# Sparse attention on one core: index keys, head weights and keys as one 328-column product with the tokens stationary

## What is computed

```python
proj = x @ w_in                                   # x: 256 x 1024, w_in: 1024 x 2120
q, k, v, iq, ik, iw = split(proj)                 # 1024, 256, 256, 512, 64, 8 columns
q, k, iq, ik = (partial_rotary(t, cos, sin) for t in (q, k, iq, ik))
iw = iw * IDX_HEADS ** -0.5
s = einsum('bqhd,bsd->bqhs', iq, ik) * 64 ** -0.5
score = einsum('bqh,bqhs->bqs', iw, relu(s))      # causal; the best 64 keys of a query are kept
_, sel = top_k(score, 64)
# softmax(q k[sel]) v[sel], then @ w_o, layer norm, squared-ReLU MLP, and the other layers
```

## Time and profile before

| | us |
|---|---|
| median of three runs | 1240.17 |
| lowest and highest | 1239.46, 1240.72 |
| the profiled execution, its own time | 1240.88 |
| span of its trace (first to last instruction) | 1239.1 |
| TensorE matmuls busy | 1229.2 (99%) |
| TensorE weight loads busy | 1051.7 (85%) |
| VectorE busy | 853.0 (69%) |
| ScalarE busy | 589.7 (48%) |
| GpSimd busy | 94.9 (8%) |

### The profile page before, as it was taken

How to read it: one execution, slowest core, us unless ns; L and a number is a source line. 1 busy time by engine, 2 the same in 40 slices (tenths; PEclk the granted TensorE clock), 3 DMA queues, 4 the chain that set the end, 5 groups by cost and what they waited for, 6 DMA issues and landing times.

```text
span 1239.1 us, 18755 instructions
## 1 busy us (share of the span) xinstructions
PE 1229.2 (99%) x7999; PEld 1051.7 (85%) x7999; DVE 853.0 (69%) x918; ACT 589.7 (48%) x713; POOL 94.9 (8%) x226
## 2 busy tenths in 40 slices
PE   9999999999999999999999999999999999999998
PEld 8888888888888888888988888888898888888887
DVE  6887776666765776667776676668587666766675
ACT  5774444334753544344664444345472544444434
POOL 5441000001000200000101000001000100000000
PEclk9999999999999999999999999999999999999999
DMA  8424655555634756554625656555554247655642
GB/s 282 171 70 161 214 191 186 201 182 154 216 116 136 257 186 203 181 193 147 221 76 182 218 180 202 182 192 204 181 192 158 103 150 237 199 185 189 200 140 102
DMA packets 127234, 221.03 MB, mean 178 GB/s; under 512 B 7048, under 2 KB 91296, under 8 KB 127152
## 3 DMA queue, kind: packets, MB, share of 16 engines
q1 hardware_dynamic: 124128, 209.83, 50.6%
q0 software_dynamic: 3024, 10.01, 2.6%
HBM read 218.77 MB, written 1.05 MB: 177 GB/s over the span
## 4 chain that ended last, share of the span: by engine, by line
PE 95%; ACT 1%; DVE 1%; DMA 1%; POOL 1%; issue 1%; SPq 0%; POOLq 0%
PE ps L794 20%; PE ps L622 18%; PE ps L796 10%; PE ps L599 10%; PE ps L600 10%; PE ps L601 10%; PE ps L762 5%; PE ps L810 2%; PE ps L706 2%; PE ps L1034 1%; PE ps L981 1%; PE ps L1149 1%; DVE wlo L1875 1%; PE ps L881 1%; PE ps L929 1%
## 5 line engine op out<-in xcount | busy, mean ns | idle before, releaser
L1875 DVE TENSOR_TENSOR wlo<-raw,whi 128x2048 fp32r<-128x2048 f32 (+3 forms) x203 | 452.4, 2242 | 174.8 <-ACT whi L1423 173.6
L1423 ACT ACTIVATE whi<-raw 128x2048 fp32r<-128x2048 f32 (+3 forms) x203 | 376.7, 1869 | 73.7 <-DMA raw<-in_hgrn_w_in 21.5
L794 PE MATMUL ps<-xhl,whi 128*128 128x512 f32 x1088 | 271.8, 392 | 0.0
L794 PEld LDWEIGHTS ps<-xhl,whi 128*128 128x128 f32 x1088 | 198.4, 188 | 37.4
L622 PE MATMUL ps<-whi,xhl 128*128 128x512 f32 (+1 forms) x736 | 182.7, 380 | 0.8 <-ACT xhl L1440 0.6
L599 PE MATMUL ps<-whi,hh 128*128 128x512 f32 x432 | 168.8, 391 | 0.0
L600 PE MATMUL ps<-whi,hl 128*128 128x512 f32 x432 | 168.6, 390 | 0.0
L601 PE MATMUL ps<-wlo,hh 128*128 128x512 f32 x432 | 168.1, 389 | 0.0
L796 PEld LDWEIGHTS ps<-xhl,wlo 128*128 128x128 f32 x1088 | 148.4, 190 | 10.6
L622 PEld LDWEIGHTS ps<-whi,xhl 128*128 128x128 f32 x736 | 130.7, 188 | 26.0 <-issue 0.9
L796 PE MATMUL ps<-xhl,wlo 128*128 128x256 f32 x1088 | 151.7, 282 | 0.0
(11 more groups left out here) (344 smaller groups left out, 1334.2 us busy)
## 6 DMA issues: line engine op xcount, KB each, us to landing
raw<-in_ffn_w_in SPq DMA_DIRECT2D x40, 1024.0 KB, 5.1
raw<-in_mlp_w_up SPq DMA_DIRECT2D x32, 1024.0 KB, 5.4
raw<-in_mlp_w_down SPq DMA_DIRECT2D x32, 1024.0 KB, 4.9
raw<-in_ffn_w_down SPq DMA_DIRECT2D x22, 1024.0 KB, 4.9
raw<-in_hgrn_w_in SPq DMA_DIRECT2D x16, 1024.0 KB, 5.5
raw<-in_b_w_in SPq DMA_DIRECT2D x12, 1024.0 KB, 5.2
raw<-in_ple_w_gate SPq DMA_DIRECT2D x8, 1024.0 KB, 6.0
raw<-in_a_w_in SPq DMA_DIRECT2D x6, 1024.0 KB, 5.7
```

The costliest lines, as they stand in the source:

```text
L794: mm(bank(b + f), w[0][:, kk, P * f : P * f + P], xhl[:, kk, :, :].rearrange("p a n -> p (a n)"), start=(kk == 0), stop=False)
L1423: a.activation(whi[:, slot, 0:w], raw[:, slot, 0:w], ACT.Copy).then_inc(s["hi_done"], 1)
L1875: v.tensor_tensor(wlo[:, slot, 0:w], raw[:, slot, 0:w], whi[:, slot, 0:w].bitcast(F32), ALU.subtract).then_inc(s["lo_done"], 1)
```

## The change

The small chunk and the key chunk are put together and cut in two by rows: chunks 4 and 5 now hold rows 0 to 511 and 512 to 1023 of 328 columns (256 of keys, 64 of index keys, 8 of head weights), 4 x 328 = 1312 values a partition each. Each is brought by two transfers, 256 columns and 72 columns. TensorE has the tokens stationary and 328 columns moving, so that index keys and head weights come out by token; the small product of before, its two transposes and two copies go. ScalarE and VectorE copy the three parts of a token tile (index keys, head weights with their factor, keys) out of the accumulators, one tile each, and GpSimd no longer scales the head weights. The places of the sines and of the parts in ScalarE's and VectorE's lists change a little, and VectorE now waits for `index_rotated` before it makes the low parts of chunks 8 to 10.

```diff
-        chunk("dsa_small", rows_of(a_in, 0, KD, A_IK, A_SMALL), KD, A_SMALL)
-        chunk("dsa_k", rows_of(a_in, 0, KD, A_K, FG), KD, FG)
+        for q in range(2):
+            chunk("dsa_k", [rows_of(a_in, 4 * q, 4, A_K, FG), rows_of(a_in, 4 * q, 4, A_IK, A_SMALL)], 4, K_COLS)
...
 (GpSimd)
-            pool.wait_ge(s["small_out"], 1)
+            pool.wait_ge(s["small_act"], 1)
+            pool.wait_ge(s["small_dve"], 1)
             rotate_both(ikw[:, :, 0:A_HD].unsqueeze(2), 1)
             for tt in range(TT):
                 last = g.tensor_copy(ikdup[:, tt, :, :], ikw[:, tt, 0:A_HD].unsqueeze(1).broadcast_to([P, 2, A_HD]))
-            step(last)
-            g.tensor_scalar(ikw[:, :, A_HD:A_SMALL], ikw[:, :, A_HD:A_SMALL], float(IDX_HEADS**-0.5), None, ALU.mult).then_inc(s["index_rotated"], 1)
+            last.then_inc(s["index_rotated"], 1)
...
 (TensorE)
-            n = first["dsa_small"]
-            take(n)
-            w = weights(n, KD, A_SMALL)
-            for part, (w_part, x_part) in enumerate(((0, xh), (1, xh), (0, xl))):
-                for kk in range(KD):
-                    last = mm(ps[0:A_SMALL, 0, 0:SEQ], w[w_part][:, kk, :], x_part[:, kk, :],
-                              start=(part == 0 and kk == 0), stop=(part == 2 and kk == KD - 1))
-            last.then_inc(s["w_done"], 1)
             n = first["dsa_k"]
-            take(n)
...
-            rows(n, KD, FG, 0, KD, [(0, slice(0, FG), bank(4, FG))], within=turn_small, at=(0, KD - 1))
-            rows(n, KD, FG, 0, KD, [(1, slice(0, FG), bank(5, FG))]).then_inc(s["w_done"], 1)
-
-            pe.wait_ge(s["small_out"], 1)
+            key_tiles = [(tt, slice(0, K_COLS), bank(4 + tt, K_COLS)) for tt in range(TT)]
+            by_rows(n, 4, K_COLS, 0, KD, key_tiles)
+            take(n + 1)
+            rows(n + 1, 4, K_COLS, 4, KD, key_tiles[0:1]).then_inc(s["keys0_done"], 1)
+            rows(n + 1, 4, K_COLS, 4, KD, key_tiles[1:2]).then_inc(s["w_done"], 1)
...
 (ScalarE)
-            until(first["dsa_small"])
+            until(first["dsa_iq"] + 3)
             for w, (sn, cs) in enumerate(((sinA, cosA), (sinM, cosM))):
                 act.wait_ge(s["angle_done"], w + 1)
                 a.activation(sn[:, :, :], cs[:, :, :], ACT.Sin)
                 a.activation(cs[:, :, :], cs[:, :, :], ACT.Sin, scale=0.5).then_inc(s["sines_done"], 1)
-                until(first["dsa_k"])
+                until(first["dsa_k"] + w)
...
-            act.wait_ge(s["w_done"], first["dsa_small"] + 1)
-            a.activation(smallT[:, :], ps[0:A_SMALL, 0, 0:SEQ], ACT.Copy).then_inc(s["small_copied"], 1)
-            act.wait_ge(s["small_turned"], 1)
-            a.activation(ikw[:, :, :], bank(1, TT * A_SMALL).rearrange("p (t c) -> p t c", t=TT), ACT.Copy).then_inc(s["small_out"], 1)
             until(first["dsa_q"] + 1)
-            act.wait_ge(s["w_done"], first["dsa_k"] + 1)
+            act.wait_ge(s["keys0_done"], 1)
+            a.activation(ikw[:, 0, 0:A_HD], ps[:, 4, FG : FG + A_HD], ACT.Copy)
+            a.activation(ikw[:, 0, A_HD:A_SMALL], ps[:, 4, FG + A_HD : K_COLS], ACT.Copy, scale=float(IDX_HEADS**-0.5)).then_inc(s["small_act"], 1)
...
 (VectorE)
             angles(0, sinA, cosA, 0, ROT)
-            until(first["dsa_small"])
+            until(first["dsa_k"])
             tables(0, cosA)
             angles(1, sinM, cosM, ROT, M_HALF)
             dve.wait_ge(s["w_done"], first["dsa_iq"] + 4)
             v.tensor_copy(kvi[:, 1, 512:1024], bank(3)).then_inc(s["iq_dve"], 1)
-            until(first["dsa_k"])
+            until(first["dsa_k"] + 1)
             tables(1, cosM)
...
-            dve.wait_ge(s["w_done"], first["dsa_k"] + 1)
+            dve.wait_ge(s["w_done"], first["dsa_k"] + 2)
+            v.tensor_copy(ikw[:, 1, 0:A_HD], ps[:, 5, FG : FG + A_HD])
+            v.tensor_scalar(ikw[:, 1, A_HD:A_SMALL], ps[:, 5, FG + A_HD : K_COLS], float(IDX_HEADS**-0.5), None, ALU.mult).then_inc(s["small_dve"], 1)
             v.tensor_copy(kvi[:, 1, 0:FG], bank(5, FG)).then_inc(s["k_dve"], 1)
+            dve.wait_ge(s["index_rotated"], 1)
             until(first["dsa_v"])
-            dve.wait_ge(s["index_rotated"], 1)
```

More of the change, by code:

```diff
@@ L33 @@
 A_SMALL = A_IN - A_IK
+K_COLS = 256 + A_SMALL
 ROT = A_HD // 4 // 2
@@ L254, in _ @@
                 dst = raw[:, n % RING, 0 : k * cols].rearrange("p (k c) -> p k c", k=k)
[L255 to L258, removed]
+                at = 0
+                for piece in src if isinstance(src, list) else [src]:
+                    sp.dma_start(dst[:, :, at : at + piece.shape[-1]], piece).then_inc(s[f"raw_landed{n % RING}"], 16)
+                    at += piece.shape[-1]
             for i, (tt, c0, c1) in enumerate(LAST_PARTS):
@@ L284, in build @@
         bias = work[:, :, 0, :]
-        smallT = work[0:A_SMALL, 0, 0, :]
         logit = buf[6][:, :].rearrange("p (e n) -> p e n", e=2)
@@ L1049, in _ @@
             nc.tensor.transpose(ps[:, 6, 0:V_ROWS], vrow[:, :], ident[0:V_ROWS, 0:V_ROWS]).then_inc(s["vrow_turned"], 1)
-            n = first["dsa_small"]
-            take(n)
-            w = weights(n, KD, A_SMALL)
-            for part, (w_part, x_part) in enumerate(((0, xh), (1, xh), (0, xl))):
-                for kk in range(KD):
-                    last = mm(ps[0:A_SMALL, 0, 0:SEQ], w[w_part][:, kk, :], x_part[:, kk, :],
-                              start=(part == 0 and kk == 0), stop=(part == 2 and kk == KD - 1))
-            last.then_inc(s["w_done"], 1)
-            n = first["dsa_k"]
-            take(n)
[L1061 to L1066, removed]
-            rows(n, KD, FG, 0, KD, [(0, slice(0, FG), bank(4, FG))], within=turn_small, at=(0, KD - 1))
-            rows(n, KD, FG, 0, KD, [(1, slice(0, FG), bank(5, FG))]).then_inc(s["w_done"], 1)
-            pe.wait_ge(s["small_out"], 1)
+            n = first["dsa_k"]
+            key_tiles = [(tt, slice(0, K_COLS), bank(4 + tt, K_COLS)) for tt in range(TT)]
[3 more added lines that the diff above has]
+            rows(n + 1, 4, K_COLS, 4, KD, key_tiles[1:2]).then_inc(s["w_done"], 1)
             pe.wait_ge(s["iq_act"], 1)
@@ L2207, in _ @@
             until(first["dsa_q"] + 1)
-            dve.wait_ge(s["w_done"], first["dsa_k"] + 1)
+            dve.wait_ge(s["w_done"], first["dsa_k"] + 2)
+            v.tensor_copy(ikw[:, 1, 0:A_HD], ps[:, 5, FG : FG + A_HD])
+            v.tensor_scalar(ikw[:, 1, A_HD:A_SMALL], ps[:, 5, FG + A_HD : K_COLS], float(IDX_HEADS**-0.5), None, ALU.mult).then_inc(s["small_dve"], 1)
             v.tensor_copy(kvi[:, 1, 0:FG], bank(5, FG)).then_inc(s["k_dve"], 1)
+            dve.wait_ge(s["index_rotated"], 1)
             until(first["dsa_v"])
-            dve.wait_ge(s["index_rotated"], 1)
+            dve.wait_ge(s["small_act"], 1)
+            dve.wait_ge(s["small_dve"], 1)
             for u, (b, hs) in enumerate(INDEX_UNITS):
```

## The result

The changed kernel takes 1244.56 us (median of 6 runs, 1242.28 to 1245.88), the kernel before, on the same chip, 1240.66 us (6 runs). The ratio is 1.003, interval 1.002 to 1.004. The forecast was 1239.9 us with a range of 1238.5 to 1241.5: too low, and outside its range.

A forecast was written before the change was run, and what follows sets the result against it. TensorE, busy 99% of the span, was taken to bound the kernel. Of 1.61 us saved, 1.38 is lost waiting at chunk 5; net 0.23 off 1240.17 gives 1239.9 us, range 1238.5 to 1241.5.

The forecast's parts named there:

- The sum: Whole kernel: net 0.23 us saved at the start, taken off the 1240.17 us median, gives 1239.9 us.
- 328-column matmuls at 0.150 us, 1.61 us saved: TensorE's key work at the start: 48 new matmuls take 7.20 us in place of 8.81, if TensorE never waits.
- The wait at chunk 5, 1.38 us: TensorE near 24.67 us waits 1.38 us, as chunk 5's high part stands behind table M's sines on ScalarE.
- Net 0.23 us: At the start, of 1.61 us saved on TensorE, 1.38 is given back waiting at chunk 5.
- GpSimd in time by 1.2 us: Before the index queries' turn: GpSimd signals `index_rotated` at about 34.15 us, TensorE wants it at 35.32.
- Rival 2: GpSimd's rotation steps meet more low parts, so TensorE waits for its signal: 1240.7 to 1242.6 us; 16%.
- VectorE's delay hidden: VectorE's low parts of chunks 8 to 10, now behind `index_rotated`: up to 0.9 us of delay would be hidden.
- Rival 1: The wait at chunk 5 is absent or short, so up to 1.61 us arrives: 1238.6 us; 12%.
- Rival 3: An idle TensorE falls back to a slower clock and loses 3.1 us: 1243.0 us; 6%.
- A: Follow-up theory: TensorE's instructions arrive in pieces; a late piece stops runs of short matmuls; the instruction count sets where.

The follow-up runs named there:

- the kernel with M late and 112 waits: Changed kernel with table M's angles and sines moved behind chunk 5's parts, plus 112 instructions of already-signalled waits in the first MLP layer: 1238.90 us, ratio 0.9984.
- the kernel with 26 small matmuls after the first place: Changed kernel plus 26 unused 24-column matmuls in the first feed-forward layer, between the gaps near 333 and 955 us: 1243.80 us, ratio 1.0022.
- the one with 112 waits: Changed kernel plus sixteen already-signalled waits ahead of each of the 14 groups of the first MLP layer, 112 instructions: 1240.32 us, ratio 0.9996.
- the pair with passed waits: Already-signalled waits added in the first MLP layer: 112 instructions in the changed kernel, 1240.32 us; 56 in the kernel before, 1239.88 us.
- the run with fewer fillers: Kernel before with its idle-time transposes replaced by fewer 512-column float32 matmuls, only 8 matmuls fewer in effect: 1251.44 us, ratio 1.0083.

## Why the prediction was wrong

The step that failed is the second sentence on what bounds the kernel: "So a microsecond taken out of TensorE's list early should arrive at the end, as long as nothing else has to be waited for in its place." What had to be waited for in its place was TensorE's own code, 300 and 930 us later: gaps of 1.68 us near 333 us, where 0.91 had been, and of 1.75 us near 955 us, where there had been none, with 3.41 us at half the clock behind it. The sum has no term for this; it puts all that lies behind the start at nothing. The clue was among the rows: the earlier trace rows show 0.9 us at L981 with "issue" as releaser, a wait without a cause in the middle of a run, and the prediction cites it as proof that waits are few. Where it fell was a matter of which matmul stood at the edge of a piece, and the change moved other matmuls there.

Point by point:

- **328-column matmuls at 0.150 us, 1.61 us saved.** Right. The 48 of the kernel with M late and 112 waits take 20.41 to 33.21 us less 5.67 us for the query chunk, 7.13 us or 0.149 us each. The interpolation from rows was better than the 139 ns that the Trainium skill gives for single matmuls (TensorE: Matmul & The Clock Gate, section "Back-to-back issue gap"). The prediction's estimate from that rule, a saving of about 1.2 us, does not follow from its figures: 64 matmuls at 109 ns less 48 at 139 ns are 0.3 us.
- **The wait at chunk 5, 1.38 us.** Right in kind: 1.36 us, released by the low part of chunk 5. That the size agrees so closely is in part luck: with the same start it was 1.01 us in the kernel with 26 small matmuls after the first place, and 0.93 us in the one with 112 waits. The chain behind it was 0.3 us late throughout (high part from 23.40, not 23.07; low part to 26.24, not 25.91), and chunk 4 was ready at 21.01 us, 0.06 us ahead of its use and not 0.5.
- **Net 0.23 us.** Not settled. In the traces of before and after the index queries are turned at 35.51 us, 0.13 us later than before (35.38) and not 0.23 earlier, and the kernels are level at 90 us, to 0.1 us. In the pair with passed waits they are turned at 34.77 us (after, 112 waits) and 34.99 (before, 56 waits), 0.22 us earlier, and so it stays at 90 us. One execution differs from the next by more than the term.
- **GpSimd in time by 1.2 us.** Right in kind: its copies end at 34.66 us (forecast 34.15), 0.85 us ahead. Rival 2 did not happen.
- **VectorE's delay hidden.** Right: three low parts from 34.70 us, no new wait on TensorE up to 90 us.
- **Rival 1 (no wait, 1238.6 us).** Not the case here, but its worth is now measured: with code in place, the late table brings 1240.32 down to 1238.90 us, 1.4 us. In the two traces it is 1.57 us at 90 us. The wait that went was 0.93 us long there, so not all of the gain is the wait; 0.36 us were there before the first 328-column matmul already (20.41 and 20.77 us).
- **Rival 3 (the clock falls: 1243.0 us, 6%).** The clock fell, but not where and not for what the rival said. The 1.36 us at chunk 5 left it at 2.4 GHz; a gap of 1.75 us in short matmuls 930 us later brought it to 1.2. It cost 1.7 us, not the 3.1 taken from the start. That its time is nearest the result is chance.
- **The change by itself** is worth nearly nothing, as forecast; whether it gains or loses is not shown. With the code moved out of the way in both, it is 1240.32 beside 1239.88 us, 0.4 us slower with intervals that overlap (0.9987 to 1.0005 and 0.9982 to 0.9999); in the two traces it is 0.4 us faster.

Sum of the miss, from the profiled executions (1245.88 and 1240.88 us): 0.1 at the start, 0.8 at the first place, 0.3 near 411 us, 3.5 at the second place; 0.3 us is outside these and not traced. Shown: that TensorE stops behind the same number of its own instructions in every gap, so that the number ahead decides which matmul stands at the place; that 52 and more put back take the second gap out of the changed kernel, wherever they stand and whatever they do; and that a gap ends 2.2 to 2.5 us after the start of a q8 transfer, always the one whose turn it is by count. In the kernel before, with eight matmuls missing, a second gap appears, but its start was 5.9 us later too. That this transfer brings the very instructions that are missing is not seen directly, as no trace shows what it carries; place and count leave little else. Open: what sets the start of a transfer, why the clock fell behind some gaps and not behind others, and why with 52 or more instructions beyond the count of the kernel before both transfers start some 200 records earlier (3,995 to 4,002 in place of 4,176 to 4,223; 12,444 to 12,453 in place of about 12,655), which took the gaps away with more room than A foresaw.

## What to carry to other kernels

In a long unrolled program like this one, an edit that changes the number of instructions can bring a run of short matmuls to an edge of the code supply; look for a wait with "issue" as releaser in the middle of such a run, and for its match in the instruction queue, before costing an edit to 0.3%. To judge an edit of that size, compare it at equal count: 56 or 112 passed waits among long matmuls cost nothing that could be seen here, and moved all that stood behind them. A wait that an edit creates (chunk 5 behind the sines of table M) shows its worth only once that noise is out: with the gaps there, the medians of the two kernels differ by 0.6 us (1244.56 and 1243.98, from different groups of runs, less than their intervals can tell apart), without them by 1.4.

## What was unexpected of the hardware

- TensorE runs out of instructions: 64 matmuls of 16 columns take 0.74 us with their loads, 128 instructions or 5.8 ns each, while TensorE went on only 2.2 to 2.5 us after a piece's transfer had started, although the transfer itself took 0.9 to 1.0 us in the gaps measured.
- The clock's fall is no function of the gap's length here: it fell for 3.41 us behind gaps of 1.65, 1.75, 1.75 and 2.31 us, and stayed at 2.4 GHz behind gaps of 1.68, 1.66, 1.44 and 1.81 us, behind all shorter ones, and behind the 1.36 us at chunk 5.
- A plain float32 matmul of 512 columns, in the run with fewer fillers, took two records 0.43 us apart (14 records in 6.01 us), so 0.86 us for one matmul, against 0.236 us for one of the split products.
